# Norm factors applied to results instead of to inputs in the second block of a fused transformer kernel

## The reference

```python
def rms_norm_2(x, g):
    y = xf * lax.rsqrt(jnp.mean(xf * xf, axis=-1, keepdims=True) + EPS)
    return y * g

def hybrid_layer(x, ...):                 # second block, twice
    proj = rms_norm_2(x, norm1_g) @ w_in  # qa ka va qi ki wi qb kb vb rb gl uc
    ...
    x = x + mix
    h = rms_norm_2(x, norm2_g) @ w_up     # 1024 -> 2 x 2816
    a, b = h[..., :D_FF], h[..., D_FF:]
    x = x + (jax.nn.silu(conv(a)) * b) @ w_down

x = first_block(...)        # its last step: rms_norm(x, g_final)
for l in range(2): x = hybrid_layer(x, ...)
return rms_norm_2(x, final_norm_g)
```

## Time and profile before

| | |
|---|---|
| median of three executions | 3893.44 us |
| profiled execution, its span | 3901.72 us, 3899.9 us |
| TensorE products busy | 3515.4 us, 90% |
| VectorE busy | 2107.1 us, 54% |
| ScalarE busy | 1411.0 us, 36% |
| POOL busy | 105.8 us, 3% |
| TensorE clock granted, mean | 0.946 of full |

### The profile page before, as it was taken

The page is one execution under the profiler, slowest core; times in us unless marked ns, Lnnn a source line. Parts: engine busy times, 40 slices in busy tenths (PEclk is TensorE's granted clock), DMA queues, the critical chain, the costliest instruction groups (busy, mean ns, idle before and its releaser), DMA issues.

```text
span 3899.9 us, 45994 instructions
## 1 busy us (share of the span) xinstructions
PE 3515.4 (90%) x18072; PEld 2805.4 (72%) x18072; DVE 2107.1 (54%) x3298; ACT 1411.0 (36%) x2231; POOL 105.8 (3%) x60
## 2 busy tenths in 40 slices
PE   2999999979899989999979998888899989879997
PEld 2866778868788767667868876665688767568876
DVE  7854653355555564436346643784555259545433
ACT  2344343333223233435433322434333233533322
POOL 0000000000000000000000000310000004000000
PEclk9999999989999989999989998888899989889998
DMA  5410212111341222001212222110222222012222
GB/s 200 150 54 12 82 38 77 60 44 59 119 173 59 108 103 71 22 31 36 81 60 97 92 91 94 56 70 14 73 92 97 92 78 76 22 49 94 95 92 81
DMA packets 80832, 301.38 MB, mean 77 GB/s; under 512 B 8864, under 2 KB 8864, under 8 KB 79904
## 3 DMA queue, kind: packets, MB, share of 16 engines
q1 hardware_dynamic: 79376, 292.39, 21.2%
q10 hardware_dynamic: 1296, 6.82, 0.5%
HBM read 297.07 MB, written 2.10 MB: 77 GB/s over the span
## 4 chain that ended last, share of the span: by engine, by line
PE 58%; DVE 10%; ACT 3%; DMA 2%; issue 1%; ACTq 0%; SPq 0%; DVEq 0%
PE ps L616 16%; PE ps L618 16%; PE ps L617 16%; DMA ada_t<-ada_w 2%; DVE work L2343 2%; DVE top L2342 1%; PE ps L876 1%; DVE sumN L1813 1%; DVE split L1781 1%; ACT split L1283 1%; PE ps L660 1%; PE ps L923 1%; PE ps L918 1%; PE ps L946 1%; PE ps L671 1%
## 5 line engine op out<-in xcount | busy, mean ns | idle before, releaser
L1781 DVE TENSOR_TENSOR split<-raw,split 128x1024 fp32r<-128x1024 f32 x412 | 504.1, 1224 | 1119.8 <-ACT split L1283 1119.6
L1283 ACT ACTIVATE split<-raw 128x1024 fp32r<-128x1024 f32 x442 | 465.5, 1053 | 415.3 <-PE ps L618 311.1
L616 PE MATMUL ps<-h,split 128*128 128x512 f32 x1328 | 541.4, 408 | 31.4 <-DVE split L1781 18.7
L618 PE MATMUL ps<-h,split 128*128 128x512 f32 x1328 | 532.5, 401 | 0.0
L617 PE MATMUL ps<-h,split 128*128 128x512 f32 x1328 | 528.9, 398 | 0.0
L616 PEld LDWEIGHTS ps<-h,split 128*128 128x128 f32 x1328 | 254.2, 191 | 101.7 <-DVE split L1781 22.5
L616 PE MATMUL ps<-h_hl,split 128*128 128x512 f32 (+1 forms) x776 | 299.2, 386 | 19.3 <-DVE h_hl L1853 8.9
L617 PEld LDWEIGHTS ps<-h,split 128*128 128x128 f32 x1328 | 254.5, 192 | 64.2 <-issue 2.9
L618 PEld LDWEIGHTS ps<-h,split 128*128 128x128 f32 x1328 | 253.5, 191 | 63.4
L617 PE MATMUL ps<-h_hl,split 128*128 128x512 f32 (+1 forms) x776 | 280.1, 361 | 0.0
L618 PE MATMUL ps<-h_hl,split 128*128 128x512 f32 (+1 forms) x776 | 280.1, 361 | 0.0
(11 more groups left out here) (372 smaller groups left out, 6380.9 us busy)
## 6 DMA issues: line engine op xcount, KB each, us to landing
raw<-wstream SPq DMA_DIRECT2D x442, 512.0 KB, 3.4
ada_t<-ada_w SPq DMA_DIRECT2D x96, 512.0 KB, 4.4
ada_c<-c_in SPq DMA_DIRECT2D x3, 1024.0 KB, 4.7
x<-x_in SPq DMA_DIRECT2D x1, 3072.0 KB, 23.0
x<-x_in ACTq DMA_DIRECT2D x1, 3072.0 KB, 12.5
out<-x SPq DMA_DIRECT2D x1, 2048.0 KB, 7.2
par<-params SPq DMA_DIRECT2D x1, 1344.0 KB, 18.6
ropeA<-rope_tab ACTq DMA_DIRECT2D x2, 512.0 KB, 4.6
```

The lines of the kernel that those rows point to most:

```text
L616: nc.tensor.matmul(o, wh, a[0], start=first, stop=False)
L618: return nc.tensor.matmul(o, wl, a[0], start=False, stop=last)
L1283: nc.scalar.activation(split[:, n % SPLIT_SLOTS, 0, :], raw[:, n % RAW_SLOTS, :], copy).then_inc(hi_split, 1)
L1781: nc.vector.tensor_tensor(split[:, n % SPLIT_SLOTS, 1, :], raw[:, n % RAW_SLOTS, :], split[:, n % SPLIT_SLOTS, 0, :].bitcast(F32), ALU.sub ...
```

## The change

In the second block the products take h = gain x (high and low part) without the factor of the token. As soon as a residual chunk is written, ScalarE makes its high part with the gain and its square (`raise_chunk`), and VectorE its low part and the running sum (`raised_low`). The residual itself is one VectorE instruction that reads the bank (`take_residual`). The sums and the spread stand inside the first three slabs of the following products (`raised_products`). The spread factors are copied to SBUF by ScalarE (`take_spread`: `rs_up` for the up projection, `rs_in` for the projections), and applied later: in the feed-forward by VectorE as it takes each result from its bank (`take_scaled`; ScalarE evicts nothing there), in the projections through the rope tables (`cos2`, `sin2` are the tables times `rs_in`), through ScalarE's per-partition scale for `va`, `vb` and `wi`, and by POOL for `gl`, `uc`, `qb`, `kb` and `rb`. The gains of conv and gate do not change.

At the border of the blocks two norms meet. The product of `g_final` and `norm1` is the gain; squares are made twice, with and without `g_final`, and `second_roots` forms the second factor from the second sum. `rs_x` is the first factor; POOL multiplies x by `g_final` and `rs_x` in place (16 instructions) ahead of its first weight split. The angles and sines are computed in the down projection before, in four steps beside chunks 0 to 3. The final norm uses the same raised squares, and the result is stored chunk by chunk.

The diff, cut to what the prediction speaks of (in `ffn2` and `down` the first of two versions is ScalarE's, the second VectorE's):

```diff
-            sp.wait_ge(final_ready, DC)
-            sp.dma_start(out, x[:, :, CTX:TOK]).then_inc(stored, 16)
-            sp.wait_ge(stored, 16)
+            for k in range(DC):
+                sp.wait_ge(final_ready, k + 1)
+                sp.dma_start(out[:, k, :], x[:, k, CTX:TOK]).then_inc(stored, 16)
+            sp.wait_ge(stored, 16 * DC)
...
+            def raised_sums(i, adds):
+                norms.add()
+                added.add(adds)
+                pe.wait_ge(var_ready, norms.now(back=1))
+                pe.wait_ge(sq_summed, added.now())
+                for t in range(QT):
+                    mm = nc.tensor.matmul(ps[:, NORM_BANK, i * QT + t:i * QT + t + 1], sumR[i][:, t * P:(t + 1) * P],
+                                          col("ones"), start=t == 0, stop=t == QT - 1)
+                mm.then_inc(sums_ready, 1)
+            def raised_products(two):
+                sq.add(2 * DC if two else DC)
+                for n in range(3):
+                    w, o = open_slab(), open_acc(SEQ)
+                    for k in range(DC):
+                        if n == 0 and k == 0:
+                            wait_hl(DC - 1)
+                        elif n == 0 and k == DC - 1:
+                            wait_hl(1)
+                        elif n == 1 and k == 1:
+                            raised_sums(0, 2 * DC - 3 if two else DC - 1)
+                        elif n == 1 and k == 4 and two:
+                            raised_sums(1, 1)
+                        elif n == 2 and k == 0:
+                            norm_spread(0, 2 * QT if two else QT, signal=raised_spread)
+                        mm = product(o, w, k, own(h2)(k, (0, SEQ)), k == 0, k == DC - 1)
+                    mm.then_inc(slab_used, 1)
+            def ffn(n, raised=False):
+                if raised:
+                    raised_products(False)
...
+                first = res.n
+                raised_products(l == 0)
+                projections(IN2_INDEX[3:], {("qi", 0): first + 1, ("qi", 1): first + 2, "kgw": first + 3})
...
+            def raise_chunk(m, gains, scales):
+                res.add()
+                act.wait_ge(acc_taken, res.now())
+                xm = x[:, m, CTX:TOK]
+                if gains is not None:
+                    nc.scalar.activation(h2[:, 0, m, :], xm, ACT.Identity, scale=gains(m)).then_inc(hi_ready, 1)
+                for i, scale in enumerate(scales):
+                    dst = sumR[i]
+                    if m:
+                        squared.add()
+                        dst = sqR[squared.n % 2]
+                        act.wait_ge(sq_summed, squared.now(back=2))
+                    if scale is None:
+                        nc.scalar.activation(dst[:, :], xm, ACT.Square).then_inc(sq_ready, 1)
+                    else:
+                        nc.scalar.activation(dst[:, :], xm, ACT.Square, scale=scale(m)).then_inc(sq_ready, 1)
+            def take_spread(*dsts):
+                spreads.add()
+                act.wait_ge(raised_spread, spreads.now())
+                for i, dst in enumerate(dsts):
+                    ins = nc.scalar.activation(dst[:, :], ps[:, ACC_BANKS + i, :], copy)
+                ins.then_inc(rs_ready, 1)
...
+            def ffn2(l):
+                for m in range(FC):
+                    full.add()
+                    convs.add()
+                    pass_slab()
+                    if m == 0:
+                        roots(QT)
+                    pass_slab()
+                    if m == 0:
+                        take_spread(rs_up)
+                    res.add(2)
+                    gated(m, SEQ)
+                if l < LAYERS - 1:
+                    down(lambda m: col(f"norm1{l + 1}", m), (None,), True)
+                else:
+                    down(None, (None,), False)
+            def down(gains, scales, turns):
+                if turns:
+                    act.dma_start(pos[:, :], pos_in).then_inc(rope_in, 16)
                 for m in range(DC):
-                    for _ in range(2):
+                    for _ in range(3):
                         pass_slab()
-                    residual_term(evd, n, True, None if gate is None else mod[:, l, 5 * DC + m, gate])
+                    raise_chunk(m, gains, scales)
+                    if turns and m in (4, 5):
+                        angs.add()
+                        act.wait_ge(ang_ready, angs.now())
+                        table = (sin_t, cos_t)[m - 4]
+                        nc.scalar.activation(table[:, :], table[:, :], ACT.Sin).then_inc(trig_ready, 1)
...
+                projections(IN2_INDEX[:1], 0)
+                roots(QT)
+                if l == 0:
+                    roots(QT, QT)
+                projections(IN2_INDEX[1:2], 0)
+                take_spread(*((rs_x, rs_in) if l == 0 else (rs_in,)))
...
+            def raised_low(m, gains, sums):
+                if gains is not None:
+                    dve.wait_ge(hi_ready, his.add().now())
+                    nc.vector.scalar_tensor_tensor(h2[:, 1, m, :], x[:, m, CTX:TOK], gains(m), h2[:, 0, m, :].bitcast(F32),
+                                                   ALU.mult, ALU.subtract).then_inc(hl_ready, 1)
+                for i in range(sums):
+                    sqs.add()
+                    if m:
+                        added.add()
+                        dve.wait_ge(sq_ready, sqs.now())
+                        nc.vector.tensor_tensor(sumR[i][:, :], sumR[i][:, :], sqR[added.n % 2][:, :], ALU.add)\
+                            .then_inc(sq_summed, 1)
+                        dve.wait_ge(sq_summed, added.now())
+            def second_roots():
...
+                nc.vector.reciprocal(two, m).then_inc(var_ready, 1)
...
+            def take_scaled(dst, slab, factors):
+                res.add()
+                dve.wait_ge(slab_used, slab + 1)
+                nc.vector.tensor_tensor(dst, ps[:, (res.n - 1) % ACC_BANKS, :], factors, ALU.mult).then_inc(acc_taken, 1)
+                dve.wait_ge(acc_taken, res.now())
+            def take_residual(m, slab, gate):
+                res.add()
+                dve.wait_ge(slab_used, slab + 1)
+                o, xm = ps[:, (res.n - 1) % ACC_BANKS, :], x[:, m, CTX:TOK]
+                if gate is None:
+                    ins = nc.vector.tensor_tensor(xm, xm, o, ALU.add)
+                else:
+                    ins = nc.vector.scalar_tensor_tensor(xm, o, gate(m), xm, ALU.mult, ALU.add)
+                ins.then_inc(acc_taken, 1)
+                dve.wait_ge(acc_taken, res.now())
+            def ffn2(l):
+                w, b = COLS[f"conv_w_2{l}"][0], COLS[f"conv_b_2{l}"][0]
+                for t in ua:
+                    v(nc.vector.memset(t[:, 0:2], 0.0))
+                for m in range(FC):
+                    j = m % 2
+                    if m == 0:
+                        reciprocal_roots([(DC, [(0, SEQ)], D)])
+                    split_low()
+                    if m == 0:
+                        copied.add()
+                        dve.wait_ge(rs_ready, copied.now())
+                    take_scaled(ua[j][:, 2:SEQ + 2], FFN2_AT[l] + 2 * m, rs_up[:, :])
+                    conv(ca, ua[j], SEQ, w, b, FC, m).then_inc(conv_done, 1)
+                    split_low()
+                    take_scaled(ub[j][:, 0:SEQ], FFN2_AT[l] + 2 * m + 1, rs_up[:, :])
+                    gated(m, ub[j][:, 0:SEQ])
+                last = l == LAYERS - 1
+                down(DOWN2_AT[l], None, None if last else (lambda m: col(f"norm1{l + 1}", m)), 1, not last)
+            def down(first, gate, gains, sums, turns):
                 for m in range(DC):
-                    split_low(3)
-                    residual(evd[m % 4], (c0, n), m)
+                    split_low(2)
+                    take_residual(m, first + 3 * m + 2, gate)
+                    split_low()
+                    raised_low(m, gains, sums)
+                    if turns and m < 4:
+                        (angles, reduced, sine_angles, cosine_angles)[m]()
...
+                reciprocal_roots([(DC, [(0, SEQ)], D)])
+                results(IN2_INDEX[:1], 0)
+                if l == 0:
+                    second_roots()
+                results(IN2_INDEX[1:2], 0)
+                copied.add()
+                dve.wait_ge(rs_ready, copied.now())
                 dve.wait_ge(trig_ready, 2 * (l + 1))
-                results(IN2_INDEX[3:], 0)
+                nc.vector.tensor_tensor(cos2[:, :], cos_t[:, :], rs_in[:, :], ALU.mult).then_inc(tab_made, 1)
+                nc.vector.tensor_tensor(sin2[:, :], sin_t[:, :], rs_in[:, :], ALU.mult).then_inc(tab_made, 1)
+                dve.wait_ge(tab_made, 2 * (l + 1))
+                results(IN2_INDEX[2:], 0)
                 dve.wait_ge(acc_taken, res.now())
-                pooled[l] = (res.n + 1, tables.n)
...
+                if l == 0:
+                    pool.wait_ge(rs_ready, copied)
+                    pool.wait_ge(hl_ready, lows)
```

(48 more changed lines are left out.)

231 lines of the change are left out of this document (126 added, 105 removed).

## The result

The change takes 3792.8 us (median of four executions, 3791.3 to 3796.0) against 3893.5 for the kernel before on the same chip: ratio 0.9745, interval 0.9728 to 0.9762, 100.7 us faster. The prediction was 3805, that is 88.1 less than before, in a range of 3792 to 3824: the right direction and inside the range, at its lower edge; the gain was forecast an eighth too small.

A forecast was written before the change was run, and what follows sets the result against it. TensorE's waits at norm seams, and the lowered clock there, were taken as the loss. Gains of 22.8 (A), 19.0 (B), 17.7 (C), 19.0 (D) and 9.9 (end), less 0.3, make 88.1 us: 3805, range 3792 to 3824.

The forecast's parts named there:

- The last chunk is hidden: At the seams: chunk 8's low part is ready at 3.4 us, before the first slab needs it at 4.9; nothing waits.
- The end: Final norm and store: sums start 5.6 us earlier and storing by chunks saves 4.3 more, 9.9 us gained.
- Sums of one norm cost 1.83, a spread of four tiles 2.07: Prices in us, from the earlier trace, for the norm work left in TensorE's stream at every seam.
- Seam B: Output projection to up projection, layer 0: four slabs take 26.3 us against 45.4, 19.0 gained.
- D: The same stretch as output projection to up projection, one layer later; taken as equal, 19.0 us gained.
- Seam A: First block to second: 39.5 us against 70.9 to the fifth slab, 31.2 gained; 22.8 after POOL's turns with VectorE.
- what POOL gets: Layer 0: POOL's 16 instructions on x start 20.3 us after the first-to-second-block seam; eight pairs take 18.8 us alone.
- 3.7 of slack, less some 2 for a lower clock: Layer 0, behind `best_keys`: TensorE's 22.6 us gain plus this slack, less the clock loss, makes 24.3 in all.
- more hits in `best_keys`: POOL's five further instructions hit VectorE's operations there: up to two hits of about 1.5 us, one taken per layer.
- The turns: After the first-to-second-block seam, POOL and VectorE instructions alternate: rotations go 29.9 to 46.0 us instead of 29 to 37.
- no turns: Rival: POOL does not hold VectorE up, or its column product is cheap; sum 98 us, 3795; chance 0.15.
- C: Layer 0 to layer 1: 35.5 us against 54.9 for five slabs, 19.2 gained; 17.7 after one hit in `best_keys`.

The follow-up runs named there:

- the run with the column as a tensor: Against the changed kernel, POOL's product of x with g_final written as a product of two tensors, the column spread over 512 elements; 3783.5 us, executed once.
- The run with the factors out: Against the changed kernel, POOL's five factor products (gl, uc, qb, kb, rb) cut to one column each in both layers; 3799.3 us, ratio 0.9758 to the kernel before.

## Why the prediction was right, and by what it was short

**The mechanism held.** The last chunk is hidden, all seams run at full clock, and no split is waited for in the second block's feed-forwards: each waits once, 5.5 us for its last `g_hl`, before 5.2 (0.15 dearer was forecast). The end gave 10.5 for 9.9: its sums start 2.4 us after the last residual's mark instead of 7.8, 5.3 earlier where 5.6 was forecast, and the store by chunks brought 5.0 for 4.3.

**Sums and spread were mis-sized.** "Sums of one norm cost 1.83, a spread of four tiles 2.07" came from the earlier trace rows, where the earlier trace rows show the clock at 0.53. In the stream they take 0.95 and 1.05. Seam B in the change:

```profile
2723.21 0.95 PE L1053 MATMUL ps<-par,sumR 128*128 128x1 f32 x8
...
2729.00 1.05 PE L688 MATMUL ps<-par,rstd 128*128 128x128 f32 x8
```

Four slabs at B were through TensorE 24.1 us after the mark, where the prediction said 26.3. With 3.9 priced and 2.0 paid, that is 1.9 of the 2.1 us missing at B and at D, and the 4.2 at A up to the fifth slab (39.5 predicted, 35.3). I had the price and the clock both in hand and did not multiply them.

**Seam A, 31.2 for 22.8.** The step "what POOL gets" had the wrong start, 15.9 us after the seam instead of 20.3, the same miss. Its length, 27.0 for 26.9, was right by luck: undisturbed, a pair took 2.9 us (1.57 and 1.29) and not 2.3, so eight would take 23.4 instead of 18.8, and the turns stretched POOL's work by 3.6 us instead of the forecast 8.1. TensorE was 24.4 ahead at `qb` (before 2493.78 - 2415.91, after 2463.28 - 2409.77) where I had 22.6; the slab behind its wait took 8.2 us, at the lower clock, which ate the rest. Then the step "3.7 of slack, less some 2 for a lower clock" fell: TensorE gained 6.8 more up to `mix`. Before, the wait of 3.7 was followed by a stretch at 0.90; after, there is neither (how much of the 6.8 is the clock's is not shown):

```profile
2580.00:2613.70 33.70, 29.81 (x105) 21.20 (x104) 29.35 (x46) 15.88 (x27) 0.00 (x0) 0.90 0.18 63
```

```profile
2545.00:2576.30 31.30, 31.30 (x123) 22.83 (x122) 28.42 (x43) 15.96 (x26) 1.14 (x1) 1.00 0.25 84
```

And the 1.5 us for more hits in `best_keys` did not apply, since TensorE did not wait for VectorE's selection: that started 37.2 us after the seam instead of the forecast 47.6, 35.6 earlier than before, and grew by 3.8, so it ended 31.8 us earlier, nearly the same as the 31.2 by which the stage shrank. 1.8 at `qb`, 6.8 - 1.7 = 5.1 of slack and this 1.5 are the 8.4 by which A was short.

**The turns, half right.** By the Trainium skill (SBUF — State Buffer, SBUF: two separate sides) GpSimd and a two-input VectorE instruction exclude each other for a whole instruction. The trace and the run with the column as a tensor agree for POOL's two-input form, and not for its product with a column, beside which VectorE's products ran in 0.69 to 1.07. So a rotation took 3.5 and not the forecast 5.4. The rival *no turns* got near the total (98 for 102.0 behind seam A), and its 31.2 for A is the measured number, but not by its mechanism: some turns were taken, and the missing price was made up by the clock at which the sums and the spread ran.

**C, 18.8 for 17.7.** Up to the first `score` 21.4 were gained (19.2 and the 2.1 above); best keys grew by 3.8 us instead of the 1.5 I took as one hit per layer, and 1.2 us more were gained behind them (35.2 us to `mix` instead of 36.5). So the total is near because these misses cancel. The run with the factors out puts these instructions at 6.5 us of VectorE's time there and 4.2 of the stage.

## What to carry to other kernels

A price read at a seam carries the clock of that seam: before it goes into a sum for a stream that stays busy, look at the granted clock of its row. A wait costs its length and the slow stretch behind it, and removing it gives both back. And where two engines' paths are nearly equally long, undo both before saying that neither costs anything.

## What the hardware showed unexpectedly

- On POOL a 128x512 product with a column took 1.57 us undisturbed, the product of two tensors with the column spread out 1.03. The forecast had 1.0 for the first. The estimate by the Trainium skill's GPSIMD Engine Reference (Elementwise — side-by-side cycle accounting), 769 ns for a tight one-input loop of 512 elements, was half of what was measured.
- Behind 2.7 us of one-column fp32 products in a row the granted clock fell from 1.00 to 0.57, with TensorE busy throughout; behind 0.95 us of them, in the change, it stayed at 1.00.
- Executions of the kernel before differed by up to 13.0 us (3886.9 to 3899.9), and the traces of the variants by as much ahead of seam A, where their work is almost the same; behind it most stretches repeat to 0.4 us where nothing was changed in them. The exceptions are those between `mix` and the last result of the output projection, 136.5 to 143.9, and one C of 163.4, where the granted clock differs.
